# Weighted values as three float32r products of high and low parts, and the first chunk transposed inside the projection

## The reference

```python
scores = jnp.einsum('bqhmd,bkhmd->bhmqk', q, k).astype(jnp.float32) * ATTN_SCALE
scores = jnp.where(visible, scores + bias, -jnp.inf)
p = jax.nn.softmax(scores, axis=-1)
a = p[:, :, 0] - lam * p[:, :, 1]
return jnp.einsum('bhqk,bkhe->bqhe', a.astype(v.dtype), v)
```

## Time and profile before

| what | value |
| --- | --- |
| median of 3 runs | 1574.97 us (1574.3 to 1575.33) |
| the profiled execution | 1575.97 us |
| its span, first to last instruction | 1574.3 us |
| mean granted TensorE clock, share of 2.4 GHz | 0.984 |

### The profile page before, as it was taken

The page is one execution under the profiler, slowest core; times in us unless marked ns, Lnnn a source line. Parts: engine busy times, 40 slices in busy tenths (PEclk is TensorE's granted clock), DMA queues, the critical chain, the costliest instruction groups (busy, mean ns, idle before and its releaser), DMA issues.

```text
span 1574.3 us, 25558 instructions
## 1 busy us (share of the span) xinstructions
PE 1509.5 (96%) x8432; PEld 1293.2 (82%) x8432; DVE 928.2 (59%) x2087; ACT 859.2 (55%) x2325; POOL 680.6 (43%) x1407
## 2 busy tenths in 40 slices
PE   5999999998999999989999999899999999699997
PEld 4888888887888888868888888688888888588886
DVE  6676666676555566675555667665556657433232
ACT  5666666665555655565565555755565566321121
POOL 6655555535644433446454433655544433300000
PEclk9999999998999999999999999999999999799999
DMA  7242221153422222134322221314222110433431
GB/s 229 85 144 95 95 94 68 71 159 108 131 97 68 68 67 68 46 110 126 104 71 68 68 68 65 116 56 150 69 91 74 54 51 17 153 120 133 147 120 67
DMA packets 99431, 149.11 MB, mean 95 GB/s; under 512 B 10288, under 2 KB 79792, under 8 KB 90608
## 3 DMA queue, kind: packets, MB, share of 16 engines
q1 hardware_dynamic: 99312, 147.62, 28.7%
HBM read 103.03 MB, written 44.56 MB: 94 GB/s over the span
## 4 chain that ended last, share of the span: by engine, by line
PE 85%; DVE 5%; issue 3%; ACT 2%; POOL 2%; SPq 1%; DMA 1%; POOLq 0%; DVEq 0%; ACTq 0%
PE pab L570 42%; PE oar L640 7%; PE qkb L691 7%; PE pab L731 6%; PE qkb L731 6%; PE qkb L596 6%; PE tb L631 3%; DVE scores L1112 2%; PE tb L670 2%; PE tb L718 1%; SPq L305 1%; PE oar L612 1%; PE oar L609 1%; PE oar L611 1%; PE tb L536 1%
## 5 line engine op out<-in xcount | busy, mean ns | idle before, releaser
L570 PE MATMUL pab<-w_hi,xr 128*128 128x512 f32 x2176 | 785.6, 404 | 2.6 <-issue 2.4
L570 PEld LDWEIGHTS pab<-w_hi,xr 128*128 128x128 f32 x2176 | 413.9, 190 | 83.2 <-issue 3.6
L570 PE MATMUL pab<-w_lo,xr 128*128 128x512 f32 x1088 | 428.4, 394 | 0.0
L1316 POOL TENSOR_TENSOR dd<-dd 128x64 f32<-128x64 f32 x340 | 118.0, 347 | 459.3 <-DVE dd L1097 459.3
L570 PEld LDWEIGHTS pab<-w_lo,xr 128*128 128x128 f32 x1088 | 207.8, 191 | 33.2
L691 PE MATMUL qkb<-kp,q 128*128 128x512 f32 (+3 forms) x656 | 186.9, 367 | 21.6 <-DVE kp L1060 19.8
L828 ACT ACTIVATE fb<-pab 128x256 f32<-128x256 f32 x68 | 26.1, 385 | 274.4 <-PE pab L570 274.4
L1112 DVE CUSTOM_DVE_ANT_0 scores<-qkb,bias 128x512 f32<-128x512 f32 (+4 forms) x136 | 84.9, 625 | 153.1 <-PE qkb L691 153.1
L883 ACT ACTIVATE scores<-scores,nmx 128x128 f32<-128x128 f32 (+16 forms) x136 | 156.9, 1164 | 16.4 <-DVE nmx L1122 16.4
L691 PEld LDWEIGHTS qkb<-kp,q 128*128 128x128 f32 x656 | 120.6, 190 | 53.6 <-DVE kp L1060 21.2
L640 PE MATMUL oar<-vv,at 128*128 128x128 f32 x1104 | 152.5, 277 | 1.9 <-ACT at L849 1.9
(11 more groups left out here) (143 smaller groups left out, 2625.1 us busy)
## 6 DMA issues: line engine op xcount, KB each, us to landing
xr<-xs SPq DMA_DIRECT2D x51, 1024.0 KB, 5.3
xs<-xr SPq DMA_DIRECT2D x17, 1024.0 KB, 3.9
w_raw<-in_w_in SPq DMA_DIRECT2D x48, 256.0 KB, 5.8
mix<-mx SPq DMA_DIRECT2D x68, 128.0 KB, 2.2
bias<-mix SPq DMA_DIRECT2D x17, 512.0 KB, 5.0
w_raw<-in_x_prompt SPq DMA_DIRECT2D x16, 512.0 KB, 3.9
scores<-in_x_prompt SPq DMA_DIRECT2D x16, 512.0 KB, 4.2
out<-vv SPq DMA_DIRECT2D x16, 512.0 KB, 3.0
```

The lines of the kernel that those rows point to most:

```text
L570: last = mm(pab[:, b, :], x, w[:, kt, 512 * b:512 * b + 512], start=(kt == 0 and part == 0 and w is w_hi), stop=(kt == KT - 1 and part == 1))
L1316: g.tensor_tensor(o[:, :, 0, :], ref, c[:, :, 0, :], sub)
```

## The change

Weights and values of the value product are split in high and low parts, and each block takes three float32r products in two instructions: high weights times high and low values side by side (256 columns of PSUM), and low weights times high values (128 columns, added to the first half). VectorE makes the low weights from PSUM (`low_weights`), and adds the two halves (`sum_values`) to `osum`, from which squares and `finish` now read. GpSimd splits the values (`split_values`), ScalarE copies them from PSUM to `vn`, which has two slots and own transfers out. The transposes of the first chunk move in front of the last piece (kt = 7) of b = 0 of the projection, and ScalarE's copy of them in front of its wait for the projection. In the sample's step, VectorE subtracts the pieces 0, 1 and 3 of the next head's b = 0 weights behind `split_qk` and no longer ahead of it. Setup buffers that shared memory with `vv`, `at` and `junk` lie elsewhere. The core of the diff:

```diff
+        vh = sb("vh", [P, SLOTS, 2, VD], f32r)
+        vn = sb("vn", [P, 2, VD])
+        osum = sb("osum", [P, VD])
-        at = sb("at", [P, 2, 512])
+        at = sb("at", [P, 2, 2, 512], f32r)
...
                     if b == 0 and kt == 6:
                         transpose_recurrence(h, t, first)
+                    if b == 0 and kt == KT - 1 and before:
+                        chunk_transposes(*before, 0)
...
             def attend(h, t, first, following):
-                if t == SAMPLE:
-                    need(pe, h, "cache_in", 64)
+                need(pe, h, "v_split", t + 1 + (t == SAMPLE))
+                apart(pe)
+                need(pe, h, "o_sum", t)
...
-                        last = mm(oar[:, 0, 0:VD], at[0:n, u % 2, b:b + P], vv[0:n, slot, :],
-                                  start=(c == 0 and j == 0), stop=(c == len(chunks) - 1 and j == len(blocks) - 1))
+                        end = c == len(chunks) - 1 and j == len(blocks) - 1
+                        high, low = at[0:n, u % 2, 0, b:b + P], at[0:n, u % 2, 1, b:b + P]
+                        both = vh[0:n, slot].rearrange("p a c -> p (a c)")
+                        if c == 0 and j == 0:
+                            if end:
+                                mm(oar[:, 0, VD:2 * VD], high, both[:, VD:2 * VD], start=True, stop=True)
+                                mm(oar[:, 0, 0:VD], high, both[:, 0:VD], start=True, stop=False)
+                            else:
+                                mm(oar[:, 0, 0:2 * VD], high, both, start=True, stop=False)
+                            last = mm(oar[:, 0, 0:VD], low, both[:, 0:VD], start=False, stop=end)
+                        else:
+                            mm(oar[:, 0, 0:VD], low, both[:, 0:VD], start=False, stop=False)
+                            last = mm(oar[:, 0, 0:2 * VD], high, both, start=False, stop=end)
...
             def attention_columns(h, t, weights):
+                pa = pab[:, 0, :]
+                weights(0)
                 need(act, h, "proj_done", t + 1)
...
-                F(vv[:, slot_of(t), :], pa[:, 2 * P:3 * P], ACT.Copy)
+                need(act, h, f"v_out{t % 2}", 16 * (t // 2))
+                apart(act)
+                need(act, h, "v_split", t)
+                F(vn[:, t % 2, :], pa[:, 2 * P:3 * P], ACT.Copy).then_inc(S["v_nat"], 1)
...
-                    F(at[:, u % 2, 0:w], tb[:, u % 2, 0:w], ACT.Copy).then_inc(S["t_evac"], 1)
+                    F(at[:, u % 2, 0, 0:w], tb[:, u % 2, 0:w], ACT.Copy).then_inc(S["at_hi"], 1)
...
-                need(act, h, "pv_done", t + 1)
-                F(junk[:, 0:P], oar[:, 0, 0:P], ACT.Square, scale=rsum[:, 0:1], accum_out=ssq[:, 0:1])
+                need(act, h, "o_sum", t + 1)
+                F(junk[:, 0:P], osum[:, :], ACT.Square, scale=rsum[:, 0:1], accum_out=ssq[:, 0:1])
...
+            def low_weights(h, t, c):
+                u = at_use(h, t, c)
+                w = P * len(blocks_of(t, c))
+                need(dve, h, "at_hi", at_index[t, c] + 1)
+                tt(at[:, u % 2, 1, 0:w], tb[:, u % 2, 0:w], at[:, u % 2, 0, 0:w].bitcast(f32), ALU.subtract
+                   ).then_inc(S["t_evac"], 1)
+
+            def sum_values(h, t):
+                need(dve, h, "pv_done", t + 1)
+                v.tensor_reduce(osum[:, :], oar[:, 0, 0:2 * VD].rearrange("p (a c) -> p c a", a=2), AX.X, ALU.add
+                                ).then_inc(S["o_sum"], 1)
...
                     if t == SAMPLE:
-                        split_weights(h, 1, (4, 5, 7))
-                        if h < HEADS - 1:
-                            split_weights(h, 0, (0, 1, 3))
+                        for c in range(4):
+                            low_weights(h, t - 1, c)
+                            if c in (1, 3):
+                                split_weights(h, 1, (4, 5) if c == 1 else (7,))
+                    if before and t < SAMPLE:
+                        for c in range(len(chunks_of(before[1]))):
+                            low_weights(*before, c)
                     split_qk(h, t)
+                    if before:
+                        sum_values(*before)
+                    if t == SAMPLE and h < HEADS - 1:
+                        split_weights(h, 0, (0, 1, 3))
                     biased_scores(h, t, before)
...
             combine(HEADS - 1, SAMPLE, HEADS - 1)
+            low_weights(HEADS - 1, SAMPLE, 0)
             split_weights(HEADS - 1, 0, (0, 1, 3, 4, 5, 7))
+            sum_values(HEADS - 1, SAMPLE)
             finish(HEADS - 1, SAMPLE)
...
+            def split_values(h, t):
+                for j, (raw, slot) in enumerate(((vn[:, t % 2, :], slot_of(t)), (vc[:, :], CACHE_SLOT))):
...
+                    g.tensor_copy(vh[:, slot, 0, :], raw).then_inc(S["v_hi"], 1)
+                    need(pool, h, "v_hi", t + 1 + j)
+                    g.tensor_tensor(vh[:, slot, 1, :], raw, vh[:, slot, 0, :].bitcast(f32), ALU.subtract
+                                    ).then_inc(S["v_split"], 1)
...
                     gates(h, t)
+                    split_values(h, t)
                     if t == SAMPLE:
                         split_weights(h, 0, LO_POOL)
```

75 lines of the change are left out of this document (43 added, 32 removed).

## The result

The changed kernel takes 1683.22 us (1681.24 to 1683.65, four runs), the kernel before 1575.15 (1574.3 to 1575.35) beside it: a ratio of 1.0685, 95% interval 1.0666 to 1.0703, 108 us slower. Forecast were 1615, with a range up to 1634: the sign was right, the size was not. The profiled execution of after has a span of 1679.5 us at a mean clock of 0.978 (before 0.984).

What follows compares the result with a forecast made beforehand. TensorE, busy for 96% of the span, was taken to bound the kernel. Steps of heads 1 to 3 (22.8), first head (17.5), boundaries (-3.6) and end (3) summed to +40 us: 1615 us, 8-in-10 range 1594 to 1634.

Steps and rivals of the forecast that it cites:

- the sum of the halves: VectorE's sum behind the low keys makes squares, scales and decay later; mostly covered in long steps, 0.6 us per head.
- The link in the steps: In heads 1 to 3, value products wait for VectorE's subtraction behind the scan: 2.4 us per head, steps 12 to 15.
- the third chunks: Mid-step, TensorE can't bridge copy and subtraction: full third chunks lose 0.3 us each, 1.2 per head in steps up to 15.
- The first head: x_normalise stands ahead of the subtractions, so value products start 1.94 us behind the scan: 17.5 us with the other terms.
- The products: Two short instructions per block cost about 0.229 us instead of 0.223: +3 us, or 0.65 per head.
- Rival 3: Value products paid at column rate: -28 us instead of +3, time 1584 us; chance 0.05.
- The moved transposes: First-chunk transposes inside the projection save nothing and add waits: 1.5 us (steps 5 to 11) plus 1.2 (1 to 4) per head.
- The boundaries: Moving three weight splits behind the low keys wins 8.4 us per boundary, mostly lost to new waits: net -1.2 each, -3.6 in all.
- rival 1: TensorE's clock falls at boundary waits and the first head's late steps, 2 us each, some eight times: 1631 us; chance 0.12.
- The second wait forecast: At each boundary, TensorE waits 3.1 us at the recurrent scores and weight piece 2.
- Rival 2: Faster: the boundaries' 8.4 us each come back whole, -25 us, time 1563 us; chance 0.10.
- The end: Last head's later decayed keys and late sum delay finish and x_low, for which the epilogue waits: +3 us (0 to 5).

Runs made afterwards that it cites:

- e11: Changed kernel with the sum in PSUM, no subtraction (low product reads the high weights), and first-chunk transposes and their copy moved back: 1583.4 us.
- e7: Changed kernel with the sum in PSUM and without VectorE's subtraction, the low product reading the high weights again: 1600.1 us.
- e1: Changed kernel with the sum of the two halves kept in PSUM instead of SBUF, nothing else: 1644.0 us.
- e14: Kernel before, with four chained ScalarE copies ahead of the squares to delay them, finish still reading PSUM: 1586.7 us.
- e9: Kernel before, with ScalarE copying the value products' output to SBUF ahead of its squares and finish reading that copy: 1587.7 us.
- e10: Changed kernel with sum in PSUM and no subtraction, each 256-column product but a chunk row's first made two of 128: 1642.2 us.
- e6: Kernel before, with only the first-chunk transposes moved into the next projection and ScalarE's copy of them moved forward: 1590.8 us.
- e3: Kernel before, with three of the next head's six VectorE weight splits moved behind the low keys in the sample's step: 1572.4 us.
- e8: Kernel before, with all six VectorE weight splits of the sample's step behind the low keys and the biased scores: 1568.9 us.
- e12: Kernel before, with two VectorE weight splits in the gap behind the low keys and four behind the biased scores: 1568.5 us.
- e15: Kernel before, two weight splits behind the low keys, four behind the biased scores, ScalarE's first two high parts ahead of decay exponentials: 1566.1 us.

## Why the prediction was wrong

The medians make a ladder: before 1575.1; with the products, splits and sum in PSUM 1583.4 (e11), +8; with the moved transposes 1600.1 (e7), +17; with the subtraction 1644.0 (e1), +44; with the sum in SBUF 1683.2, +39.

**The step that failed** is the sum of the halves: "In long steps ScalarE and GpSimd have the time for it", 0.6 us per head, 2.4 in all. With `osum` in SBUF it measured 39 more than with it in PSUM. I priced the sum's lateness and never asked what moving the output from PSUM to SBUF does to the instruction that reads it. In the kernel before, lateness alone cost 12 (e14), the place alone 13 (e9).

Where each part of the ladder falls, against the forecast (profiled executions, by the starts of the projections; steps are 1 to 15, a boundary is the sample's step and the next head's first; 0.4 us ahead of step 1 are left out):

| us over before | first head, steps | heads 1 to 3, steps | three boundaries | end |
| --- | --- | --- | --- | --- |
| e11: products, split of the values, order of the weight splits, sum in PSUM | 1.5 | 7.5 | -2.5 | 1.0 |
| e7 less e11: moved transposes | 3.9 | 11.8 | 0.7 | -0.3 |
| e1 less e7: subtraction | 11.7 | 12.2 | 13.4 | 7.1 |
| after less e1: sum in SBUF | 1.3 | 31.8 | 2.3 | 1.4 |
| after | 18.4 | 63.3 | 13.9 | 9.2 |
| forecast | 17.5 | 22.8 | -3.6 | 3 |

Heads 1 to 3 lost 21.1 us each in their steps where 7.6 were forecast, and 10.6 of the difference is the sum in SBUF. In the first head it costs almost nothing; why is not shown.

**The link in the steps** was right in size for heads 1 to 3: 4.1 us per head, forecast 2.4 and 1.2 for the third chunks. Little of it shows as a wait: in steps 1 to 15 of these heads the value products wait for the subtraction for 0.25 us at step 15, and in two steps for 0.38 and 0.27 at the third chunk. The first transposes of step 15, head 3, began 0.15 us behind their chunk, and the value products 0.63 us behind the end of the scan at 1406.84; forecast were 0.15 and 0.76. Timelines of TensorE and VectorE after, answering to the earlier trace rows:

```profile
1404.80 0.63 PE L629 MATMUL tb<-ident,scores 128*128 128x128 f32 x4 [0.39 <-DVE scores L1172]
...
1407.47 0.39 PE L659 MATMUL oar<-vh,at 128*128 128x256 f32 x1 [0.25 <-DVE at L1124]
```

```profile
1406.42 0.42 DVE L1135 TENSOR_TENSOR_SCAN dd<-ones,lf 128x128 f32<-128x128 f32 x1
1406.76 0.66 DVE L1124 TENSOR_TENSOR at<-tb,at 128x512 fp32r<-128x512 f32 x1
```

The first head came out at +18.4 us in steps 1 to 15, against 17.5, but partly by luck: the subtraction cost 11.7 there, where 16.2 were counted, and the moved transposes, which the sum left out for this head, 3.9. In step 11 the scan ends at 244.32 and the products start 1.83 later; forecast was 1.94.

```profile
246.15 0.39 PE L659 MATMUL oar<-vh,at 128*128 128x256 f32 x1 [0.79 <-DVE at L1124]
```

**The products** were right in kind: low to high start 0.06 us apart and high to low 0.17, together 0.231 per block, forecast 0.229. From the timeline of TensorE after, step 15 of head 3:

```profile
1408.04 0.22 PE L662 MATMUL oar<-vh,at 128*128 128x128 f32 x1
1408.10 0.34 PE L663 MATMUL oar<-vh,at 128*128 128x256 f32 x1
1408.27 0.22 PE L662 MATMUL oar<-vh,at 128*128 128x128 f32 x1
```

In the steps of heads 1 to 3 the whole of e11 costs 2.5 us per head, where 0.65 for the products and 0.6 for the late sum were counted; how this divides between the products, the split of the values and the sum is not shown. Rival 3 is refuted by e10.

**The moved transposes** were forecast at 2.7 us per head in heads 1 to 3 and cost 3.5 (e6) to 3.9 there: short by about 1 per head. The first head's 3 to 4 us weren't in the sum at all.

**The boundaries** were wrong in sign: forecast -1.2 each, measured +3.7, +4.2 and +6.0 over the sample's step and the next head's first. Without the subtraction they come to -0.6 each (e7), so it is the link that turns the sign, at 4.5 us each where 2.4 were counted. Two things weren't in the sum. First, GpSimd's weight split lies over VectorE's, the same collision as above: the two rows of VectorE and the one of GpSimd show a split of 1.69 us (the 512-column subtraction takes 0.68 in most places) that ends 0.55 behind GpSimd's, in front of the subtractions. GpSimd was held up as well: its piece takes 1.27 us in half of its 16 places and 3.25 here, while VectorE's combination and two splits, back to back until 1078.56, take their usual time.

```profile
1078.81 1.69 DVE L1015 TENSOR_TENSOR w_lo<-w_raw,w_hi 128x512 fp32r<-128x512 f32 x1
1080.43 1.27 DVE L1124 TENSOR_TENSOR at<-tb,at 128x512 fp32r<-128x512 f32 x2
```

```profile
1076.70 3.25 POOL L1297 TENSOR_TENSOR w_lo<-w_raw,w_hi 128x512 fp32r<-128x512 f32 x1 [10.95 <-ACT w_hi L803]
```

So the value products wait for 3.21 us rather than 2.1. Second, the clock: TensorE's granted clock falls to its lower level, 1.2 GHz, after this wait, and stays there for 6.3 us; a block takes 0.43 us there in place of 0.23. So rival 1 came true at the boundaries, and not in the first head, whose late steps (such as 231 to 331 us) ran at a granted clock of 1.00. It is no new cost, though: over the three boundaries the trace has the lower level for 27 us after and for 24 before. What failed is the 2 us per boundary that the sum counted as regained.

```profile
1081.16 0.58 PE L659 MATMUL oar<-vh,at 128*128 128x256 f32 x1 [3.21 <-DVE at L1124]
```

The window behind it (stretch, length, busy times, then clock, DMA share, GB/s):

```profile
1081.16:1087.50 6.34, 6.34 (x30) 6.34 (x30) 2.89 (x5) 1.94 (x4) 4.95 (x11) 0.50 0.94 284
```

The second wait forecast came at the recurrent scores: 3.74 us at 1101.81, forecast 3.1.

```profile
1101.81 2.93 PE L603 MATMUL qkb<-kq 128*128 128x128 f32 x12 [3.74 <-DVE kq L1179]
```

The 6.29 us of the earlier trace rows went, as forecast, but waits of 0.74, 3.21, 3.74 and 0.91 us at this boundary took their place, 8.6 in all. Rival 2 is refuted, and not for the link alone: the change's order of the splits by itself, in the kernel before, gives 3 of the 25 us (e3), other orders 6 to 9 (e8, e12, e15).

**The end**: the wait at the second transposes of the epilogue grew from 2.44 to 5.4 us, +3 as forecast. The stall of the last head's sample step, which costs as much as at the boundaries, was left out of the sum: 9 in all, 7 of them the subtraction's.

The medians miss the forecast by 68 us, the profiled executions by 65 (the one after was 2 us below its median, the one before 1 above). Of these 65, the sum in SBUF in the steps of heads 1 to 3 is 32, the boundaries 17, the end 6, the first head 1; the other 9 are the 3 us per head by which e11's part, the move and the link each came out somewhat above their terms in heads 1 to 3, and they are not traced to single waits.

## What to carry to other kernels

When a change moves an operand between PSUM and SBUF, look at every instruction that reads it: if VectorE then has both tensors in SBUF, list what GpSimd runs at that time, and at the times to which the change itself shifts it. Two small costs that meet on one instruction are not a sum; run them together as well as singly. A wait of 6 us at a boundary where three engines split the next weights is worth what the next-late piece leaves of it, here 1 to 3 us, so find that piece first.

## What the hardware showed beside this

- A finish caught by a GpSimd multiply ends 0.15 us behind it. One that starts in the multiply's last 0.08 us meets GpSimd's next instruction and ends 0.15 us behind that, 0.84 us behind the first. In e9 36 of the 52 caught finishes are of this second kind.
- A short float32r product costs 0.087 us more where one of 256 columns becomes two of 128 (e10).
- VectorE's tiny `nmx` (128x2, one tensor, in and out in SBUF) is caught too, and was in the kernel before: 52 of its 68 start with GpSimd quiet and take 0.167 us, 15 start inside the multiply of the queries, take 1.12 us in the mean and end 0.02 to 0.03 us behind it. ScalarE's exponentials wait for `nmx`. I have not tried to move it.
